# Two layers in one kernel: branch and query orders changed, two experts' weights asked for earlier, norm weights put on turned rows

## The chip, the core and the metric

The kernel runs on one core of one Trainium2 chip. A core has TensorE (matrix products), VectorE, ScalarE and GpSimd (elementwise work), SyncE (issues transfers), an on-chip memory of 128 partitions, eight accumulation banks (PSUM) that TensorE writes, and 16 DMA engines. The engines run their own instruction streams in order and wait for each other by semaphores. The metric is the time of one execution in microseconds (us) on the device; of several runs the median is given.

## The reference, cut to what matters

The program is two layers on 512 tokens of width 1024, in float32. The first layer is a block with a convolution branch, a block-sparse attention, an attention to a memory, and a gated feed-forward part; the change does not touch it. The second layer is this one:

```python
h = rms_norm(x, norm1_g)
z, xbc, dt_raw, q, k, v, g_ssd, g_att = split(h @ w_in)
xbc = silu(conv(xbc, 4 taps) + conv_b);  xs, bm, cm = split(xbc)
dt = softplus(dt_raw + dt_bias);  a = -exp(a_log)
# chunks of 128 tokens, 4 groups of 8 heads: sums of dt * a, states, y_diag + y_off + xs * d_skip
y_ssd = rms_norm(y * silu(z), per group) @ w_ssd_out
y_att = window_attention(rope(rms_norm(q)), rope(rms_norm(k)), v, sinks) @ w_attn_out
x = x + (sigmoid(g_ssd) * y_ssd + sigmoid(g_att) * y_att) @ w_out
h2 = rms_norm(x, norm2_g)
# router: one of 8 groups, the best 2 of its 8 experts; 64 experts
y = sum over the 2 experts of weight * (silu(h2 @ w_gate) * (h2 @ w_up)) @ w_down     # width 256
out = x + y
```

`rms_norm(x, g)` is `x / sqrt(mean(x^2) + eps) * g`, so the factor `g` (one number for each of the 1024 columns) can be put on rows that are already scaled by their root, before or after they are turned.

## The kernel before, in words

All dense products are made from three products of rounded halves: a weight `w` is split into a rounded high part and a rounded rest, and so are the activations; `product` (L512 to L515) adds high x high, high x low and low x high. A "tile" is 8 such products of 128x128 by 128x512, so 24 matmuls. ScalarE rounds the high part of a piece of weights (`one_hi`, L2156), VectorE subtracts it for the low part (`one_lo`, L1260). Both are done ahead of use, in the fixed order of the list `parts`: `highs.upto(e, n)` and `lows.upto(e, n)` bring the rounding up to part n at the place in the engine's program where they stand. There is no scheduler: the order on each engine is the order of the code in the functions `tensor`, `vector`, `scalar`, `pool` and `sync`. PSUM banks are taken in turn, and TensorE waits for whoever has to empty a bank.

The second layer on TensorE: tiles `bm0` to `bm3`; the product for dt (a 128-column piece), its turning by four transposes (L826); tiles `cm0` to `cm3`; the sums of dt * a over a chunk (L833 to L835). Then four groups g: tiles `xs{g}` 0 to 3, each followed by a turning of the tile before (`xs_rows`, L843), the rows of z, and the chunks' products (L870, L881, L920); the last chunk of a group is handled after the first xs tile of the next (`turn`, L851). Each bm, cm and xs tile passes ScalarE (L2335, scale and bias), VectorE (L1507, three taps) and ScalarE again (L2340, Silu). dt passes VectorE (L1578, copy), TensorE, VectorE (L1582) and ScalarE (L2408 to L2414, softplus in three functions, and an exponential), then VectorE. `chunk_rows` (L1654 to L1675) and `finish` on VectorE, and `finish` (L2426, the square) and `turn` (L2431) on ScalarE close a chunk.

Then q0, q1 and kv: row blocks i = 0 to 3 of 128 tokens, each over four quarters u of the weights, with a bank for each i; ScalarE copies q0 and q1 out (L2498), VectorE the rest (L1754). The angles of the rotary part are made on VectorE and their sine on ScalarE (L2490). Gate tiles `gs`, attention, output products `so` and `ao`, and the last projection `oo` (out in two halves of columns, L1927 adds it to X) follow.

The last stage is the experts. Each of the 64 experts gets 64 places for tokens; two experts make a block, so there are 32 blocks. The rows of h2 are written to memory (`h2d`) and gathered by an indirect transfer; TensorE turns them (L1197), VectorE (L2092) and ScalarE (L2663) copy a half each, and TensorE multiplies by gate and up weights (L1218) and by down weights (L1241). Weights come straight from memory, 2 MB of gate and up and 1 MB of down for an expert, into six places each (`GUs`, `DNs`); `gates_in(n)` and `downs_in(n)` in `sync` ask for them. `gates_in(0)` waits for the last projection's last products, `("oo", 3, 1)`; from expert 6 on, it waits for the block that last used the place. Expert 5's gate weights also wait for the routing's results. In `pool`, `row_3` (L2820) multiplies a row block of h2 by the gains of the norm and writes it out.

The lines that the change touches stand in these functions:

## Time and profile before

| | us |
|---|---|
| median of 3 runs | 2140.6 (2140.24 to 2140.8) |
| the profiled execution | 2140.07, of it 2138.2 span |
| TensorE busy | 1992.2 (93%) |
| VectorE busy | 1019.0 (48%) |
| ScalarE busy | 723.0 (34%) |
| GpSimd busy | 230.2 (11%) |
| chain that ended last | TensorE 67%, DMA 16%, VectorE 11% |

The span is the time from the first to the last instruction of the profiled execution. A busy share is an average over all stages. Rows of the timeline give the start and the length of one instruction or of a run of like ones, and in brackets how long the engine had been idle and what ended that. Overlapping matmuls are pipelined: their starts give the pace. Windows give the granted clock of TensorE as a share of 2.4 GHz.

### The profile page before, as it was taken

The page shows a single profiled execution, that of the slowest core. Times are in us where ns is not written, and L with a number is a line of the kernel's source. Part 1 is how long each engine was busy: PE and PEld are TensorE (multiplying, and loading weights), DVE is VectorE, ACT ScalarE, POOL GpSimd, SP SyncE. Part 2 cuts the span into 40 slices and gives each one's busy share as a digit, 9 for nine tenths or more (in the row PEclk, how much of TensorE's full clock was granted, in tenths as well). Part 3 has the DMA queues.
Part 4 walks back from the last instruction along what each step waited for, and adds up shares of the span by engine and source line. Part 5 has one row for each costly group of instructions (what it writes and reads, how often), then busy time and mean ns, then how long its engine had stood idle before and what let it go on. Part 6 is the DMA issues. An engine that isn't in the chain of part 4 may idle for free.

```text
span 2138.2 us, 23312 instructions
## 1 busy us (share of the span) xinstructions
PE 1992.2 (93%) x9626; PEld 1422.7 (67%) x9626; DVE 1019.0 (48%) x1596; ACT 723.0 (34%) x1156; POOL 230.2 (11%) x273
## 2 busy tenths in 40 slices
PE   7999999999999999899999999999987988888886
PEld 6777788888888888777787766678883332332222
DVE  4466534447666523678888457654353111111113
ACT  5353423235444412555554325652231110010000
POOL 2000000002000001101111141200023111111110
PEclk9999999999999999999999999999997999999999
DMA  7241123243222332332223221122429999999995
GB/s 267 89 137 61 59 83 114 79 165 122 99 99 99 118 118 99 107 126 94 75 99 123 88 79 40 60 99 79 148 103 411 422 423 424 423 424 421 419 412 212
DMA packets 56858, 380.46 MB, mean 178 GB/s; under 512 B 12936, under 2 KB 13192, under 8 KB 23856
## 3 DMA queue, kind: packets, MB, share of 16 engines
q1 hardware_dynamic: 38304, 339.23, 40.9%
q0 software_dynamic: 17872, 38.68, 5.1%
q8 instruction: 76, 1.25, 0.2%
q10 hardware_dynamic: 576, 1.05, 0.1%
q14 instruction: 30, 0.25, 0.0%
HBM read 378.82 MB, written 27.89 MB: 190 GB/s over the span
## 4 chain that ended last, share of the span: by engine, by line
PE 67%; DMA 16%; DVE 11%; ACT 3%; POOL 1%; issue 1%; SPq 0%; DVEq 0%; POOLq 0%; ACTq 0%
PE PS L513 17%; PE PS L515 17%; PE PS L514 17%; DMA AR<-in_wexp 15%; PE PS L1218 5%; PE PS L976 3%; DVE rf L1260 1%; PE PS L1241 1%; DVE AR L1625 1%; DVE AR L1507 1%; DVE AR L1618 1%; PE PS L1028 1%; PE PS L1058 1%; ACT rf L2156 1%; POOL AR L2685 1%
## 5 line engine op out<-in xcount | busy, mean ns | idle before, releaser
L513 PE MATMUL PS<-rf,rf 128*128 128x512 f32 (+1 forms) x2008 | 766.2, 382 | 20.6 <-DVE rf L1260 16.7
L514 PE MATMUL PS<-rf,rf 128*128 128x512 f32 (+1 forms) x2008 | 754.6, 376 | 0.0
L515 PE MATMUL PS<-rf,rf 128*128 128x512 f32 (+1 forms) x2008 | 754.6, 376 | 0.0
L1260 DVE TENSOR_TENSOR rf<-AR,rf 128x1024 fp32r<-128x1024 f32 (+1 forms) x224 | 285.6, 1280 | 365.4 <-ACT rf L2156 365.4
L513 PEld LDWEIGHTS PS<-rf,rf 128*128 128x128 f32 x2008 | 380.3, 189 | 97.0 <-DVE rf L1260 15.3
L515 PEld LDWEIGHTS PS<-rf,rf 128*128 128x128 f32 x2008 | 380.2, 189 | 68.6
L514 PEld LDWEIGHTS PS<-rf,rf 128*128 128x128 f32 x2008 | 380.6, 190 | 67.2 <-issue 1.2
L2156 ACT ACTIVATE rf<-AR 128x1024 fp32r<-128x1024 f32 (+1 forms) x224 | 244.1, 1100 | 265.9 <-PE PS L515 212.5
L1218 PE MATMUL PS<-AR 128*64 128x512 f32 x1024 | 272.9, 644 | 51.3 <-DMA AR<-in_wexp 50.0
L1218 PEld LDWEIGHTS PS<-AR 128*64 128x64 f32 x1024 | 86.3, 147 | 232.2 <-issue 160.0
L2101 DVE TENSOR_TENSOR AR<-AR,PS 128x256 f32<-128x256 f32 x32 | 13.5, 421 | 360.8 <-ACT AR L2674 360.8
L1241 PE MATMUL PS<-AR 128*64 128x512 f32 x512 | 116.9, 598 | 16.5 <-DVE AR L2105 16.5
L2674 ACT ACTIVATE AR<-PS 128x256 f32<-128x256 f32 x32 | 12.3, 384 | 298.3 <-PE PS L1218 298.3
L1241 PEld LDWEIGHTS PS<-AR 128*64 128x64 f32 x512 | 33.9, 136 | 79.0 <-issue 54.8
L976 PE MATMUL PS<-AR 128*128 128x512 f32 x160 | 70.7, 596 | 0.0
L1507 DVE SCALAR_TENSOR_TENSOR AR<-PS,AR 128x511 f32<-128x511 f32 (+2 forms) x72 | 53.8, 747 | 18.1 <-ACT AR L2335 16.5
L2680 ACT ACTIVATE AR<-PS 128x512 f32<-128x512 f32 x32 | 19.1, 597 | 127.1 <-PE PS L1241 127.1
L2836 POOL DMA_INDIRECT AR<-h2d,IA x32 | 32.7, 1023 | 268.1 <-PE PS L1227 248.1
L2685 POOL TENSOR_SCALAR AR<-AR 128x1 f32<-128x1 f32 (+1 forms) x46 | 24.6, 536 | 322.5 <-ACT AR L2308 119.2
L976 PEld LDWEIGHTS PS<-AR 128*128 128x128 f32 x160 | 29.7, 190 | 35.7 <-issue 35.6
L2109 DVE COPY AR<-PS 128x512 f32<-128x512 f32 x32 | 22.1, 692 | 65.3 <-PE PS L1241 65.3
L1197 PEld LDWEIGHTS PS<-AR 128*128 128x128 f32 x256 | 28.1, 143 | 32.7 <-issue 25.1
(331 smaller groups left out, 1791.6 us busy)
## 6 DMA issues: line engine op xcount, KB each, us to landing
AR<-in_wexp SPq DMA_DIRECT2D x62, 2048.0 KB, 35.9
AR<-in_wpack SPq DMA_DIRECT2D x123, 1024.0 KB, 5.0
AR<-in_wexp SPq DMA_DIRECT2D x68, 1024.0 KB, 38.2
AR<-acud POOLq DMA_DIRECT2D x16, 512.0 KB, 4.0
AR<-ya SPq DMA_DIRECT2D x4, 1024.0 KB, 8.7
bvec<-bv POOLq DMA_DIRECT2D x1, 2560.0 KB, 16.0
AR<-in_x SPq DMA_DIRECT2D x4, 512.0 KB, 7.3
AR<-bvec POOLq DMA_DIRECT2D x8, 256.0 KB, 2.9
```

The source lines that it names most:

```text
L513: e.i.matmul(o, ws[0], xs[0], start=start, stop=False)
L514: e.i.matmul(o, ws[0], xs[1], start=False, stop=False)
L515: return e.i.matmul(o, ws[1], xs[0], start=False, stop=stop)
L976: m = e.i.matmul(PS[:, b, :], w[:, d, :], YT[:, d, :], start=d == 0, stop=d == 15)
L1197: m = e.i.transpose(PS[:, b, 128 * k:128 * k + 128], XB[:, s, 512 * hf + 128 * k:512 * hf + 128 * k + 128], ident)
L1218: m = e.i.matmul(PS[CAP * j:CAP * j + CAP, b, :], xt[:, k, CAP * j:CAP * j + CAP], w[:, k, :], start=k == 0, stop=k == 7)
L1241: m = e.i.matmul(PS[CAP * j:CAP * j + CAP, b2[hf], :], hd[:, q, CAP * j:CAP * j + CAP], w[:, q, 512 * hf:512 * hf + 512], start=q == 0, st ...
L1260: e.i.tensor_tensor(rounded(p.place + p.width, p.width), src, rounded(p.place, p.width).bitcast(F32), ALU.subtract).then_inc(*tick("w_lo", ...
L1507: e.i.scalar_tensor_tensor(out=y[:, q:512], in0=b[:, 0:512 - q], scalar=cp("conv_w", 24 * (3 - q) + tix), in1=y[:, q:512], op0=ALU.mult, o ...
L2156: e.i.activation(rounded(p.place, p.width), area(p.chunk.place + p.off, p.width), ACT.Copy).then_inc(*tick("w_hi", p.key))
L2685: e.i.tensor_scalar(ss, ss, 1.0 / width, EPS, ALU.mult, ALU.add).then_inc(*tick("p_out", (key, "eps")))
L2836: e.i.indirect_dma_start(XB[:, s, :], None, dram["h2d"], bass.IndirectOffsetOnAxis(ap=IA[:, 128 + blk:129 + blk], axis=0), bounds_check=51 ...
```

## The change

Six places change.

- On TensorE, tile `cm0` moves ahead of the turning of dt, and `rows` (q0, q1, kv) asks for the bank of a row block when it comes to it, not for all four at the start.
- On VectorE, the copy of dt's product moves ahead of the fourth bm tile's taps, and the rest of dt's steps are spread over cm0 and cm1. On ScalarE, softplus moves from ahead of cm0 to behind it, and the exponentials of the sums (L2420) from behind cm3 to behind the second xs tile.
- In groups 1 to 3, both engines round the third xs piece right behind the first xs tile; ScalarE then turns before it squares.
- The sine moves behind the copies of q0, and two more pieces of the gate weights are rounded ahead of kv's copies.
- The gates and downs of expert 0 are asked for after `("ao", 7)`, the last products before the last projection, and those of expert 1 after the last rounded weights. The places of the experts' weights are laid out anew, over memory that is out of use by then.
- GpSimd no longer multiplies h2 by the norm's gains (four operations and a transfer of 0.5 MB go). VectorE and ScalarE multiply the turned rows by them instead, where they copied; ScalarE does this in four operations for each block.

```diff
@@ rows (tensor)
-                bs = []
-                for i in range(n):
-                    b, was = banks.take((name, i), back(i))
-                    bs.append(b)
-                    if was:
-                        e.wait_ge(*at(*was))
+                bs = [banks.take((name, i), back(i)) for i in range(n)]
...
-                    for i in range(n):
+                    for i, (b, was) in enumerate(bs):
                         c = slice(128 * i, 128 * i + 128)
+                        if was and u == 0:
+                            e.wait_ge(*at(*was))
@@ tensor
             m.then_inc(*tick("acc", "dt"))
+            conv_tile("cm", 0, 20)
             b, was = banks.take("dtt", ("v_out", "dtb"))
...
-            for j in range(4):
+            for j in range(1, 4):
                 conv_tile("cm", j, 20 + j)
@@ vector
+                if j == 3:
+                    e.wait_ge(*at("acc", "dt"))
+                    e.i.tensor_copy(D0, ps("dt")).then_inc(*tick("v_out", "d0"))
                 conv_taps("bm", j, 16 + j, BT[:, j, :])
-            e.wait_ge(*at("acc", "dt"))
-            e.i.tensor_copy(D0, ps("dt")).then_inc(*tick("v_out", "d0"))
...
             for j in range(4):
                 lows.upto(e, min(PART["cm", j] + 4, PART["xs0", 0] + (0 if j < 3 else 3)))
                 conv_taps("cm", j, 20 + j, CT[:, j, :])
+                if j == 0:
+                    e.wait_ge(*at("acc", "dtt"))
+                    e.wait_ge(*at("rows"))
+                    e.i.tensor_tensor(cut(DT, 4), cut(ps("dtt"), 4)[:, :, 0:32], h32("dt_bias"), ALU.add).then_inc(
+                        *tick("v_out", "dtb"))
+                if j == 1:
+                    steps()
...
                     if j == 0 and g:
+                        lows.upto(e, base + 4)
                         chunk_rows(g - 1, 3)
...
-                lows.upto(e, min(PART["kv", u] + 4, PART["gs0", 0]))
+                lows.upto(e, min(PART["kv", u] + 4, PART["gs0", 0] + 2))
...
-            e.wait_ge(*at("p_out", ("h2", 3)))
             e.i.tensor_scalar(CNT, ps("count")[:, 0:64], -float(CAP), 0.0, ALU.add, ALU.max).then_inc(*tick("v_out", "cnt"))
...
-                e.i.tensor_copy(xt[:, 0:4, :], cut(ps(("xt", blk, 0)), 4)).then_inc(*tick("v_out", ("xt", blk, 0)))
+                e.i.tensor_tensor(xt[:, 0:4, :], cut(ps(("xt", blk, 0)), 4), g4, ALU.mult).then_inc(
+                    *tick("v_out", ("xt", blk, 0)))
@@ scalar
+                    if j == 1 and g == 0:
+                        sums_raised()
                     if j == 0 and g:
+                        highs.upto(e, base + 4)
+                        turn(g - 1, 2)
                         finish(g - 1, 3)
-                        turn(g - 1, 2)
...
-            e.wait_ge(*at("v_out", "ang"))
-            e.i.activation(SIN, R1, ACT.Sin).then_inc(*tick("a_out", "sin"))
-            e.i.activation(COS, R1, ACT.Sin, scale=0.5).then_inc(*tick("a_out", "cos"))
...
+                if s == 0:
+                    ahead("q1", 0)
+                    e.wait_ge(*at("v_out", "ang"))
+                    e.i.activation(SIN, R1, ACT.Sin).then_inc(*tick("a_out", "sin"))
+                    e.i.activation(COS, R1, ACT.Sin, scale=0.5).then_inc(*tick("a_out", "cos"))
...
-                e.i.activation(xt[:, 4:8, :], cut(ps(("xt", blk, 1)), 4), ACT.Copy).then_inc(*tick("a_out", ("xt", blk, 1)))
+                for q in range(4):
+                    m = e.i.activation(xt[:, 4 + q, :], ps(("xt", blk, 1))[:, 128 * q:128 * q + 128], ACT.Copy,
+                                       scale=cp("norm2_g", 4 + q))
+                m.then_inc(*tick("a_out", ("xt", blk, 1)))
@@ pool
-            e.wait_ge(*at("v_out", ("ga2", 15)))
-            e.i.dma_start(GB, dram["gains"][2:3, :].to_broadcast([128, 1024])).then_inc(*tick("gains", 2, 16))
...
                 e.wait_ge(*at("a_out", ("hx", i)))
-                e.wait_ge(*at("gains", 2))
-                e.i.tensor_tensor(XR[i], XR[i] if i < 3 else SQ3, GB, ALU.mult).then_inc(*tick("p_out", ("h2", i)))
-                e.wait_ge(*at("p_out", ("h2", i)))
                 e.i.dma_start(dram["h2d"][128 * i:128 * i + 128, :], XR[i]).then_inc(*tick(f"st{i}", "h2", 16))
@@ sync
-                e.wait_ge(*at("acc", ("gu", n // 2 - 3) if n > 5 else ("oo", 3, 1)))
+                if n == 0:
+                    e.wait_ge(*at("acc", ("ao", 7)))
+                elif n == 1:
+                    e.wait_ge(*at("w_hi", ("oo1", 1)))
+                    e.wait_ge(*at("w_lo", ("oo1", 1)))
+                else:
+                    e.wait_ge(*at("acc", ("gu", n // 2 - 3) if n > 5 else ("oo", 3, 1)))
```

The order of instructions shows three places. The first is ScalarE from the fourth bm tile to the second cm tile. `rf<-AR` is a rounding of weights, `AR<-PS,AR` the entry of a conv tile, `AR<-AR 128x512` its Silu; the rows of 128x128 and 128x32 are dt's. Before:

```order
L2335 ACTIVATE AR<-PS,AR 128x512 [waits s_acc]
L2340 ACTIVATE AR<-AR 128x512 [waits s_v_out]
L2408 ACTIVATE AR<-AR 128x128 [waits s_v_out]
L2410 ACT_TABLE_LOAD
L2410 ACTIVATE AR<-AR 128x128 [waits s_a_out]
L2412 ACT_TABLE_LOAD
L2412 ACTIVATE AR<-AR 128x128 [waits s_a_out]
L2414 ACT_TABLE_LOAD
L2414 ACTIVATE AR<-AR 128x32 [waits s_rows]
L2156 ACTIVATE rf_1024<-AR 128x1024
L2335 ACTIVATE AR<-PS,AR 128x512 [waits s_acc]
L2340 ACT_TABLE_LOAD
```

In the changed kernel, whose lines are numbered some 8 higher (L2421 is L2408 before):

```order
L2164 ACTIVATE rf_1024<-AR 128x1024
L2343 ACTIVATE AR<-PS,AR 128x512 [waits s_acc]
L2348 ACTIVATE AR<-AR 128x512 [waits s_v_out]
L2421 ACTIVATE AR<-AR 128x128 [waits s_v_out]
L2423 ACT_TABLE_LOAD
L2423 ACTIVATE AR<-AR 128x128 [waits s_a_out]
L2425 ACT_TABLE_LOAD
L2425 ACTIVATE AR<-AR 128x128 [waits s_a_out]
L2427 ACT_TABLE_LOAD
L2427 ACTIVATE AR<-AR 128x32 [waits s_rows]
L2343 ACTIVATE AR<-PS,AR 128x512 [waits s_acc]
L2348 ACT_TABLE_LOAD
```

The softplus steps and their three tables now stand behind the first cm tile's Silu, and a rounding and that tile stand ahead of them.

The second place is ScalarE at the boundary between groups 0 and 1, from the Silu of the first xs tile (128x512 behind a table) to the Silu of the second. L2426 (L2437) is the last chunk's square, L2431 (L2442) a turned chunk's copy. Before:

```order
L2340 ACTIVATE AR<-AR 128x512 [waits s_v_out]
L2426 ACTIVATE AR<-AR 128x512 [waits s_v_out]
L2431 ACTIVATE AR<-PS 128x4x128 [waits s_acc]
L2156 ACTIVATE rf_1024<-AR 128x1024 [waits s_w_in1]
L2335 ACTIVATE AR<-PS,AR 128x512 [waits s_acc]
L2340 ACTIVATE AR<-AR 128x512 [waits s_v_out]
```

In the changed kernel:

```order
L2348 ACTIVATE AR<-AR 128x512 [waits s_v_out]
L2164 ACTIVATE rf_1024<-AR 128x1024 [waits s_w_in1]
L2442 ACTIVATE AR<-PS 128x4x128 [waits s_acc]
L2437 ACTIVATE AR<-AR 128x512 [waits s_v_out]
L2343 ACTIVATE AR<-PS,AR 128x512 [waits s_acc]
L2348 ACTIVATE AR<-AR 128x512 [waits s_v_out]
```

The rounding has gone from behind the square to ahead of it, and the turned chunk's copy too.

The third place is SyncE's queue from the first of the experts' transfers to the seventh expert's; 128x4096 are gates, 128x2048 downs. Before:

```order
L2916 DMA AR<-in_wexp 128x4096 [waits s_acc]
L2916 DMA AR<-in_wexp 128x4096
L2925 DMA AR<-in_wexp 128x2048 x2
L2916 DMA AR<-in_wexp 128x4096 x2
L2925 DMA AR<-in_wexp 128x2048 x2
L2916 DMA AR<-in_wexp 128x4096
L2925 DMA AR<-in_wexp 128x2048 x2
L2916 DMA AR<-in_wexp 128x4096 [waits s_v_out]
L2916 DMA AR<-in_wexp 128x4096 [waits s_acc]
```

In the changed kernel (L2936 is `gates_in`, L2945 `downs_in`):

```order
L2936 DMA AR<-in_wexp 128x4096 [waits s_acc]
L2945 DMA AR<-in_wexp 128x2048
L2936 DMA AR<-in_wexp 128x4096 [waits s_w_lo,s_w_hi]
L2945 DMA AR<-in_wexp 128x2048
L2936 DMA AR<-in_wexp 128x4096 [waits s_acc]
L2936 DMA AR<-in_wexp 128x4096
L2945 DMA AR<-in_wexp 128x2048 x2
L2936 DMA AR<-in_wexp 128x4096
L2945 DMA AR<-in_wexp 128x2048 x2
L2936 DMA AR<-in_wexp 128x4096 [waits s_v_out]
L2936 DMA AR<-in_wexp 128x4096 [waits s_acc]
```

Experts 0 and 1 now have waits of their own, and the wait for the last projection stands ahead of expert 2. The waits for the routing (`s_v_out`, expert 5) and for block 0 (`s_acc`, expert 6) stand where they stood.

## Rows read from the trace of the kernel before

**Rows 1.** The page, part 4: shares of the chain that ended last, by engine.
```profile
PE 67%; DMA 16%; DVE 11%; ACT 3%; POOL 1%; issue 1%; SPq 0%; DVEq 0%; POOLq 0%; ACTq 0%
```

**Rows 2.** Windows: from:to, length, each engine's busy us, granted clock, DMA share, GB/s.
```profile
1545.00:1590.00 45.00, 45.00 (x383) 45.00 (x382) 17.50 (x40) 13.42 (x17) 8.27 (x10) 1.00 0.09 34
1590.00:1635.00 45.00, 22.48 (x155) 14.07 (x154) 28.17 (x96) 6.96 (x11) 18.40 (x18) 0.62 0.96 390
1700.00:2080.00 380.00, 321.10 (x1362) 114.88 (x1360) 49.73 (x96) 36.90 (x70) 47.33 (x47) 0.95 1.01 421
```

**Rows 3.** TensorE's timeline (start, us, line, form, idle before); a row of waits.
```profile
895.99 1.12 PE L826 MATMUL PS<-AR 128*128 128x128 f32 x4 [6.23 <-DVE AR L1578]
...
1064.39 0.79 PE L513 MATMUL PS<-rf,rf 128*128 128x512 f32 x1 [2.90 <-DVE rf L1260]
...
1208.93 0.47 PE L513 MATMUL PS<-rf,rf 128*128 128x512 f32 x1 [2.86 <-ACT AR L2498]
...
1256.42 0.47 PE L513 MATMUL PS<-rf,rf 128*128 128x512 f32 x1 [2.07 <-DVE rf L1260]
...
PE PS L513 <- DVE rf L1260: 12.4, 5, 2.9
```

**Rows 4.** Windows over three stretches that follow a wait of TensorE.
```profile
895.00:902.00 7.00, 6.01 (x21) 5.00 (x22) 1.75 (x5) 5.08 (x7) 0.00 (x0) 0.66 0.00 0
1064.00:1074.00 10.00, 9.61 (x34) 7.80 (x35) 7.43 (x9) 4.16 (x4) 0.00 (x0) 0.68 0.44 138
1206.00:1215.00 9.00, 6.14 (x21) 4.86 (x21) 1.90 (x5) 3.24 (x7) 0.00 (x0) 0.81 0.29 96
```

**Rows 5.** ScalarE's timeline at dt and the cm tiles.
```profile
897.47 0.31 ACT L2408 ACTIVATE AR<-AR 128x128 f32<-128x128 f32 x1 [1.47 <-DVE AR L1582]
...
902.34 0.23 ACT L2414 ACTIVATE AR<-AR 128x32 f32<-128x32 f32 x1
...
909.36 0.78 ACT L2335 ACTIVATE AR<-PS,AR 128x512 f32<-128x512 f32 x1 [1.64 <-PE PS L515]
...
914.80 0.78 ACT L2335 ACTIVATE AR<-PS,AR 128x512 f32<-128x512 f32 x1 [1.64 <-PE PS L515]
...
918.50 3.79 ACT L2156 ACTIVATE rf<-AR 128x1024 fp32r<-128x1024 f32 x3
```

**Rows 6.** VectorE's timeline at the boundary between groups 0 and 1.
```profile
998.47 1.22 DVE L1260 TENSOR_TENSOR rf<-AR,rf 128x1024 fp32r<-128x1024 f32 x1 [2.22 <-ACT rf L2156]
```

**Rows 7.** Timeline at q0 and at the last products of kv: ScalarE, VectorE.
```profile
1206.38 0.23 ACT L2490 ACTIVATE AR<-AR 128x32 f32<-128x32 f32 x1 [2.92 <-DVE AR L1743]
...
1255.06 2.35 DVE L1260 TENSOR_TENSOR rf<-AR,rf 128x1024 fp32r<-128x1024 f32 x2
```

**Rows 8.** Timeline of the last projection and the first expert transfers.
```profile
1564.46 2.47 DVE L1927 TENSOR_TENSOR AR<-AR,PS 128x512 f32<-128x512 f32 x4
...
1624.60 10.98 SPq L2916 DMA_DIRECT2D AR<-in_wexp  x3
```

**Rows 9.** Timeline of the routing: VectorE and GpSimd.
```profile
1594.12 2.23 DVE L1941 TENSOR_SCALAR AR<-AR 128x64 f32<-128x64 f32 x1
...
1596.90 2.79 DVE L1935 SCALAR_TENSOR_TENSOR AR<-AR 128x64 f32<-128x64 f32 x1
...
1602.16 0.28 DVE L1935 SCALAR_TENSOR_TENSOR AR<-AR 128x64 f32<-128x64 f32 x1
...
1597.24 2.35 POOL L2820 TENSOR_TENSOR AR<-AR 128x1024 f32<-128x1024 f32 x1
```

**Rows 10.** Block 0 on TensorE; steps of the chain; a group of ScalarE.
```profile
1625.18 9.55 PE L1218 MATMUL PS<-AR 128*64 128x512 f32 x32 [1.29 <-DVE AR L2092]
...
1640.28 6.89 PE PS L1218 x32
...
1652.70 6.89 PE PS L1218 x32
...
L2663 ACT ACTIVATE AR<-PS 128x512 f32<-128x512 f32 x29 | 17.3, 597 | 18.5 <-PE PS L1197 18.5
```

79 lines of the change are left out of this document (43 added, 36 removed).

## The prediction

> **What bounds the kernel now.** I read the page first, then the timeline of TensorE, then the stretches by window. The chain that ended last [rows 1] is two thirds TensorE and one sixth transfers of the experts' weights. The reader should see two regimes. Up to 1591 us TensorE is busy nearly all the time, so any wait of TensorE there is worth its own length, if nothing else holds it afterwards. From 1591 us the experts' weights stream: in 1700 to 2080 the DMA share is 1.01 at 421 GB/s [rows 2], while TensorE waits. There a faster engine is worth nothing. Only a stream that starts earlier, carries less or stands still less counts. The profiled execution's 2140.07 us are a span of 2138.2 and 1.9 around it; the median of the runs, 2140.6, lies 0.5 above.
>
> The waits of TensorE that the change touches are [rows 3]: 6.2 us before the turning of dt (L826), waits for rounded weights (12.4 us in five; three of them are like the one at 1064.39, 2.9 us ahead of the third tile of a group's branch), 2.9 us before q1 (ended by ScalarE, L2498) and 2.1 us before the first gate tile. After some of them TensorE is granted half its clock (1.2 of 2.4 GHz) for a while. One minus the granted clock, times the stretch, gives the loss [rows 4]: 2.4 us after L826 (0.5 of it before the products start), 3.2 after the second group, 1.7 after q0.
>
> **dt and the cm tiles.** After the dt product TensorE (free at 895.99 - 6.23 = 889.8) now does cm0, one tile of 24 products, 5.4 us (two tiles' results reach ScalarE at 909.36 and 914.80 [rows 5]), and finds D0 copied: VectorE copies it ahead of the fourth bm tile's taps. So 6.2 + 1.9 of slow clock = 8.1 us go at the place. But ScalarE is late next. Its steps for dt (L2408 to L2414, 897.47 to 902.57, 5.1 us [rows 5]) now stand between cm0 and cm1. A turn of a tile over ScalarE, VectorE and ScalarE again takes 3.8 us (from 909.36 to 914.80 less 1.64 idle). The fourth bm tile was through ScalarE at 897.47 - 1.47 = 896.0 and is now at 896.6, with D0's copy ahead of it. From there: one rounding 1.0, cm0 3.8, dt 5.1, cm1 3.8, cm2 3.8, which is 914.1. Before, the same point, the three roundings for xs0 and z0 (3.79 us), stands at 918.50. So ScalarE gains 4.4 us and TensorE, whose cm tiles, turning and sums are done at about 913 (889.8 + 4 x 5.4 + 1.3), waits until 916 to 917 for xs0's weights, again at half clock for a while. The steps on the sums (L2420 on, with a table) move past two conv tiles and come due where ScalarE is late again, ahead of the rounding for xs0's last tile. I take 4 us, nearest the ScalarE row; the ends are 1 (the wait comes back nearly whole) and 8.
>
> Here the Trainium skill's page "ScalarE: Activation LUTs", section "What ACT_TABLE_LOAD costs", speaks against it: 1.28 us for a load and about as much again for draining, 2.66 in all. By that the three loads would make the steps 8 us and more, and the gain of this part would be about nothing, which is 2121.5 us. The whole stretch [rows 5] took 5.1 us with its three loads, so the trace shows no such second half, and the sum goes by it; the page's case has 0.02 of the chance of rival (1).
>
> **The group boundaries.** In groups 1 to 3 the rounding for the third xs tile now stands ahead of the last chunk's rows on VectorE, and ahead of the turn and the square on ScalarE. Before, VectorE idles 2.2 us for it after those rows (998.47 [rows 6]). At the place 2.9 us go three times, with 3.2 us of slow clock once. But the last chunk's rows and its square come later: VectorE stands about 1.8 us (an estimate: one small operation and one rounding of 1.0 on ScalarE) ahead of them, and 1.5 us afterwards, until ScalarE has squared and begun the next tile. So the next taps end 1 us later than before, and the fourth tile's rounding hangs on them. The wait moves one tile on. Where the clock had held (group 1) I expect nothing, even -0.3; in group 2, where TensorE had run slow for most of a tile, 2.4; in group 3 1.3; and about 1 us back for slow clock after the moved waits. Together 2.5, nearest the row in which VectorE, not TensorE, is the late one. The ends are -3 (1 us later in each group) and 12 (three times 2.9 and the 3.2).
>
> **q0, q1 and the gate tile.** ScalarE's copies of q0 stood behind a sine that waited 2.9 us for the angles [rows 7], and q1 waited for all four banks at once. Now the copies follow each row's product and q1 asks for a bank when it comes to it. Rows end 1.4 us apart (a quarter of a tile's 5.4) and a copy of this size takes 0.6 (as L2663 [rows 10]), so nothing is late: 2.9 + 1.7 of slow clock, 4.5 us. What queues behind the sine now is VectorE's rounding for q1's last quarter, due 3 x 5.4 us after q1's start. The two roundings at 1255.06 [rows 7] move ahead of the copies of k and v, under kv's products: 2.1 us, and no slow clock followed. Bounds for both together: 4 and 7.
>
> **The tail.** An expert is 128 x 6144 x 4 bytes, 3.15 MB. Two experts, 6.3 MB, now go at about 1536 (after ao7) and at 1564.5, when the last projection's weights are rounded [rows 8], where the mean is 34 GB/s over 1545 to 1590 [rows 2]. At the stream's 421 GB/s that is 14.9 us. SyncE's wait for those weights holds nothing else: all earlier loads are issued. X comes back beside the first expert; 5.2 MB in all are 12.5 us, done by 1551, ahead of the first add to X at 1564.46 [rows 8].
>
> The stream can't simply end 14.9 us earlier, because there are six buffers. The seventh expert waits for the first block's products, and those for the routing. Before: up to 1635, 45 us x 390 GB/s = 17.6 MB were moved [rows 2] of about 20.6 asked for (six experts 18.9, two rows of h2 1.0, small ones 0.7). So 3.0 MB, 7.2 us, still stood in line when block 0 ended and the seventh was asked for (the last of the three issues that begin at 1624.60 [rows 8]), and the stream never stood. After: about 14 MB are done by 1626, except for the sixth expert, which waits for the routing and is asked for at about 1620. Then nothing is left to ask for.
>
> How long nothing is left depends on the routing, and this is where the norm weights come in. Two VectorE operations on 128x64 take 2.23 and 2.79 us while GpSimd multiplies a row of h2 by the gains (1597.24, 2.35 us); the same operation takes 0.28 for the next row [rows 9]. Those multiplications go. 2.0 + 2.5 = 4.5 us leave VectorE's chain, which is what TensorE's routing products wait for. Block 0, 9.6 us from 1625.18 at a clock that rises late [rows 10], then ends at 1630.3 instead of 1634.8. The stream has no line then, and takes up again some 2 us later, at 1632.3. Before, at 1634.7, there were 7.2 us more to do. The gain is 7.2 + 2.4 = 9.6; I take 9.5. The ends: 5, if the 4.5 us of VectorE do not go, and 15, if the stream never stands.
>
> The weights on turned rows cost VectorE a product instead of a copy (0.1 us) and ScalarE four small copies instead of one of 0.6 us (L2663 [rows 10]): between +0.1 and +1.8 us (four at the price of the large one). TensorE's own pace is 12.4 us a block [rows 10], the stream's about 15.5 to 16, so this hides under the stream, and costs 0 to 2 us for all blocks together. I take 0.
>
> **The sum.** 4 + 2.5 + 4.5 + 2.1 + 9.5 = 22.6. Against the profile's own 2140.07 this gives 2117.5 us.
>
> **Rivals.** (1) The branch gives little: ScalarE and VectorE, not TensorE, set the pace from dt to the last group, so the first two parts give 1 and 0 instead of 6.5. For it speaks VectorE's idle time being ended by ScalarE [rows 6]; against it that TensorE runs nearly full between the boundaries. 2123. (2) The routing isn't shortened, since the stretched operations had another cause: 5 instead of 9.5, 2122; with (1), 2127.5. (3) The line of transfers doesn't run dry, or asked-for work spreads so that it hardly stands: 15 instead of 9.5, 2112. Against it, the six buffers. (4) The other side: scaling the turned rows. TensorE can't begin a block before ScalarE's half is written. If the four small operations and the product added more than 3.3 us to a block, TensorE would set the pace instead of the stream; from 4.2 us on, 32 blocks x 0.9 give back 29 of the 22.6 gained, and the kernel is slower, 2146. The nearest row, 0.6 us for the large copy, is against it: four such add 1.8. (5) The early transfers change nothing, because the first block isn't waiting for weights and the stream stands as long as it was relieved: the tail gives 0, 2127.
>
> **Chances.** The forecast 0.50 (own range 2112 to 2122); (1) 0.17, (2) alone or with (1) 0.10, (3) 0.11, (5) 0.07, (4) 0.03, no change at all, where two of the terms are paid back in full, 0.02. A measurement of this kernel tells about 0.2%, 4 us, from no change. Faster by more: 0.95; within: 0.02; slower: 0.03. The range, 2109 to 2128, leaves out (4), no change, and the ends of (3) and (2).
>
> **What would show it.** In the changed kernel's profile: no wait before the turning of dt, and one of 3 to 4 us before xs0's first tile; the 2.9 us waits gone from the second tile of a group and found again, as short ones, at the fourth; q1 following q0 at full clock; 3.15 MB moved after ao7, and again before the last rows; no VectorE operation of 2 us in the routing, and block 0 starting some 4.5 us sooner after the last projection; a hole in the DMA share of 4 to 8 us just before block 0 ends; from there 1.01 to the end. The forecast is wrong if the hole isn't there, if the group boundaries keep all of their 2.9 us, or if TensorE waits for ScalarE's half of the turned rows.

## The result, and the profile after

The changed kernel took 2116.9 us (median of 4 runs, 2116.5 to 2118.6) against 2140.4 for the kernel before on the same chip (2139.5 to 2140.8): a ratio of 0.9891, 95% interval 0.9877 to 0.9906. The profiled execution took 2116.47 us, its span 2114.7. On a second chip the medians were 2115.7 and 2138.6. The forecast was 2117.5, in a range of 2109 to 2128.

Where the 23.5 us of span went is read from instructions of TensorE that both traces have: the first product of the bm tiles, the first turning of a chunk in each group (L851 before, L850 here), the first scores of the attention (L1028 and L1027), which come behind kv and the first gate tiles, and the first product of the last projection. From the bm tiles to the first turning of group 0: 4.0 us less (110.5 for 114.4). From there to the same turning of group 3, three groups: 2.9 less. From there to the scores: 7.0 less. From the scores to the last projection nothing (244.9 us in both). From the last projection to the end: 9.6 less. The forecast had 4, 2.5, 6.6 and 9.5.

The chain that ended last is made up nearly as in [rows 1] (part 4 of the page):
```profile
PE 66%; DMA 17%; DVE 11%; ACT 4%; POOL 1%; issue 1%; SPq 0%; DVEq 0%; POOLq 0%; ACTq 0%
```
TensorE's timeline, at the places of [rows 3] (start, us, line, form, idle before). The lines L513, L1260 and L843 of before are L514, L1259 and L842 here.
```profile
916.19 0.54 PE L514 MATMUL PS<-rf,rf 128*128 128x512 f32 x1 [3.63 <-DVE rf L1259]
...
937.12 0.47 PE L514 MATMUL PS<-rf,rf 128*128 128x512 f32 x1 [1.32 <-DVE rf L1259]
...
999.52 0.66 PE L842 MATMUL PS<-AR 128*128 128x128 f32 x4 [1.28 <-ACT AR L2348]
...
1001.73 0.70 PE L514 MATMUL PS<-rf,rf 128*128 128x512 f32 x1 [0.89 <-DVE rf L1259]
```
No wait of 0.6 us or more stands between 868 and 916: the 6.2 us before the turning of dt are gone, and xs0's first tile now waits 3.6. Ahead of the third tile of a group nothing waits; at its end 1.3 and 0.9 us do, in all three groups. q1 and the gate tile have no wait of 0.6 us or more. What became of the slow clock of [rows 4] is seen in windows (length, busy us of the engines, granted clock, DMA share, GB/s) of the changed kernel, two at the same stretches and one, 999 to 1009, at the wait that is new:
```profile
895.00:902.00 7.00, 7.00 (x35) 5.82 (x34) 4.35 (x7) 3.29 (x6) 0.00 (x0) 1.00 0.33 97
999.00:1009.00 10.00, 8.56 (x33) 6.63 (x34) 7.43 (x9) 5.95 (x7) 0.00 (x0) 0.83 0.62 218
1206.00:1215.00 9.00, 9.00 (x41) 7.47 (x40) 2.18 (x2) 1.06 (x1) 0.00 (x0) 1.00 0.42 144
```
The clock is full after dt and after q0. It has fallen for a while after the wait ahead of xs0 (0.66 granted over 916 to 921) and after the new wait in group 1.

ScalarE's timeline answers to [rows 5]: the roundings for xs0 and z0, which began at 918.50, begin 4.7 us sooner.
```profile
901.79 1.28 ACT L2423 ACT_TABLE_LOAD   x1
...
906.33 0.23 ACT L2427 ACTIVATE AR<-AR 128x32 f32<-128x32 f32 x1
...
913.84 3.79 ACT L2164 ACTIVATE rf<-AR 128x1024 fp32r<-128x1024 f32 x3
```
The Trainium skill ("ScalarE: Activation LUTs", section "What ACT_TABLE_LOAD costs") gives 1.28 us for a load, and about as much again for draining. The first figure is what this row has to the digit. Of the second nothing is seen: the load that starts at 901.79 ends at 903.07, the next operation starts at 903.09, and the steps for dt took 5.1 us with three loads, as before.

The tail, in the windows that answer to [rows 2]:
```profile
1531.00:1577.00 46.00, 46.00 (x391) 46.00 (x391) 16.81 (x44) 13.43 (x17) 3.49 (x8) 1.00 0.39 155
1577.00:1622.00 45.00, 24.75 (x166) 14.96 (x166) 24.73 (x95) 8.82 (x18) 14.68 (x17) 0.66 0.88 343
1690.00:2060.00 370.00, 314.41 (x1345) 113.43 (x1340) 49.04 (x95) 48.87 (x138) 46.45 (x46) 0.95 1.01 421
1610.00:1615.00 5.00, 5.00 (x20) 1.72 (x18) 0.00 (x0) 0.00 (x0) 3.78 (x5) 0.72 0.59 240
1615.00:1620.00 5.00, 4.48 (x26) 1.94 (x24) 1.38 (x3) 1.53 (x5) 1.90 (x3) 1.00 0.58 141
1620.00:1625.00 5.00, 5.00 (x26) 1.73 (x24) 0.69 (x1) 0.60 (x1) 0.83 (x2) 1.00 1.00 417
```
46 us x 155 GB/s are 7.1 MB moved beside the last projection, where 34 GB/s (1.5 MB) went before. Then the stream runs full, falls to a share of 0.59 and 0.58 from 1610 to 1620 (0.41 and 0.42 of 5 us, 4.2 us lost: this is the hole), and runs at 1.01 to the end of the stretch at 2060.

Block 0, against [rows 10], with the steps that lead to it. The lines are, in this order: the last store of h2, the time from issue to landing of the one store issued in 1581 to 1583, the tokens' last operation, the fetch of block 0's rows, the turning of those rows, the block's products.
```profile
1581.47 0.53 POOL L2836 DMA_DIRECT2D h2d<-AR  x1 [0.92 <-ACT AR L2652]
...
h2d<-AR POOLq DMA_DIRECT2D x1, 512.0 KB, 14.3
...
1591.63 0.18 DVE L2014 TENSOR_SCALAR IA<-IA 128x32 int32<-128x32 int32 x1
...
1596.81 1.13 POOL L2850 DMA_INDIRECT AR<-h2d,IA  x1 [14.80 <-DVE AR L2044]
...
1605.15 1.97 PE L1196 MATMUL PS<-AR 128*128 128x128 f32 x8 [9.18 <-DMA AR<-h2d,IA]
...
1608.40 9.27 PE L1217 MATMUL PS<-AR 128*64 128x512 f32 x32 [1.28 <-issue]
```
The routing reached TensorE 4.5 us sooner after the last projection (L1158 at 1586.23; L1159 at 1604.69 before). But block 0 began only 2.8 us sooner (1608.40, where 1625.18 less 14.0 is 1611.2). The tokens were there at 1591.8, and the fetch was issued at 1596.8, when the last store had landed: it was issued at 1581.47 and took 14.3 us, so it landed at 1595.8. This is a wait that the forecast did not have. The profile names a VectorE operation as what ended the fetch's wait; in the code the fetch waits for the four stores and for the tokens, not for that operation.

The wait is not new. In the kernel before, the last store landed at 1610.6 (1599.89 and 10.7), the fetch left as long after that as it does now, and the products began 3.3 us after the turning, as they do now (1605.15 to 1608.40):
```profile
1599.89 0.59 POOL L2822 DMA_DIRECT2D h2d<-AR  x1 [0.30 <-POOL AR L2820]
1611.67 1.13 POOL L2836 DMA_INDIRECT AR<-h2d,IA  x1 [11.19 <-DVE AR L2022]
...
1621.92 1.97 PE L1197 MATMUL PS<-AR 128*128 128x128 f32 x8 [7.48 <-DMA AR<-h2d,IA]
```
So before, two chains ended nearly together at block 0: the routing on VectorE, which was free at 1624.3 to copy its half, and store, fetch and turning, whose rows were ready at 1623.9. The change took 4.1 us off the first. The second lost 2.8: the store is issued 4.4 us sooner after the last projection, but takes 3.6 longer to land, and the fetch is 1.9 shorter. In one of the runs below (six passes) the chain has the step itself, store and then fetch:
```profile
1580.92 14.21 DMA h2d<-AR
1596.18 8.18 DMA AR<-h2d,IA
```

### The profile page after: what moved, and what is told of

Its sections match the earlier page's. It is cut to its first block, busy times and chain, and to the rows that moved or that the text cites. A ratio compares the mean times of both kernels' runs of the same rounds, so it can differ in the third digit from the quotient of the medians.

```text
span 2114.7 us, 23398 instructions
## 1 busy us (share of the span) xinstructions
PE 1985.4 (94%) x9626; PEld 1418.8 (67%) x9626; DVE 1012.9 (48%) x1596; ACT 739.8 (35%) x1252; POOL 220.8 (10%) x268
## 3 DMA queue, kind: packets, MB, share of 16 engines
q10 hardware_dynamic: 576, 1.05, 0.1%
## 4 chain that ended last, share of the span: by engine, by line
PE 66%; DMA 17%; DVE 11%; ACT 4%; POOL 1%; issue 1%; SPq 0%; DVEq 0%; POOLq 0%; ACTq 0%
PE PS L514 17%; PE PS L516 17%; PE PS L515 16%; DMA AR<-in_wexp 15%; PE PS L1217 5%; PE PS L975 3%; DVE AR L1506 2%; DVE rf L1259 2%; PE PS L1240 1%; DVE AR L1631 1%; ACT rf L2164 1%; PE PS L1027 1%; PE PS L1057 1%; POOL AR L2704 1%; DVE AR L1624 1%
## 5 line engine op out<-in xcount | busy, mean ns | idle before, releaser
L514 PE MATMUL PS<-rf,rf 128*128 128x512 f32 (+1 forms) x2008 | 763.9, 380 | 13.2 <-DVE rf L1259 12.2
L1259 DVE TENSOR_TENSOR rf<-AR,rf 128x1024 fp32r<-128x1024 f32 (+1 forms) x224 | 285.8, 1281 | 368.5 <-ACT rf L2164 368.4
L514 PEld LDWEIGHTS PS<-rf,rf 128*128 128x128 f32 x2008 | 379.2, 189 | 89.0 <-DVE rf L1259 13.6
L1506 DVE SCALAR_TENSOR_TENSOR AR<-PS,AR 128x511 f32<-128x511 f32 (+2 forms) x72 | 53.8, 747 | 17.4 <-ACT AR L2343 15.7
```

The lines of the kernel that those rows point to most:

```text
L514: e.i.matmul(o, ws[0], xs[0], start=start, stop=False)
L1259: e.i.tensor_tensor(rounded(p.place + p.width, p.width), src, rounded(p.place, p.width).bitcast(F32), ALU.subtract).then_inc(*tick("w_lo", ...
L1506: e.i.scalar_tensor_tensor(out=y[:, q:512], in0=b[:, 0:512 - q], scalar=cp("conv_w", 24 * (3 - q) + tix), in1=y[:, q:512], op0=ALU.mult, o ...
```

## The experiments

Each but one is the changed kernel with an edit. The tail below is the span less the start of the last projection; without an edit it is 591.7 and 592.0 us in two profiles. The runs were spread over three chips. The kernel before had a median of 2138.2 us on the chip of the first four edits (experts late, gains, dt, all groups), 2138.6 on that of q0, the repeat, four passes and halves, and 2139.0 on that of group 1 alone, six passes and the two with the stores; its single runs spread from 2134 to 2142. Of these the changed kernel itself was run on the second only, so its stages and its tail, which agree within 0.3 us in two profiles, say more than the times do.

**Experts 0 and 1 asked for late.**
```
-                if n == 0:
-                    e.wait_ge(*at("acc", ("ao", 7)))
-                elif n == 1:
-                    e.wait_ge(*at("w_hi", ("oo1", 1)))
-                    e.wait_ge(*at("w_lo", ("oo1", 1)))
-                else:
-                    e.wait_ge(...)
+                e.wait_ge(*at("acc", ("gu", n // 2 - 3) if n > 5 else ("oo", 3, 1)))
```


> The changed kernel with experts 0 and 1 asked for where the kernel before asks for them, after the last projection's weights of the fourth row; all else stays changed. The forecast's account (the 9.6 us of the tail come from 6.3 MB moved ahead, less a hole): the stages up to the last projection stay 14.0 us sooner, the stream's line starts as before and does not run dry before block 0 ends, so the tail gives nothing: 2140.4 - 14 = 2126 to 2127, and the DMA share has no hole there. Rival (5), the first block's start sets the tail, whatever was moved ahead: block 0 still starts about 3 us sooner relative to the last projection, so the time stays at 2117 to 2119, or gives back at most half.

Measured: 2125.5 us (2125.0 to 2125.8), 0.9942 [0.9925, 0.9960] of before. The tail is 601.7 us, where before has 601.3. There is no hole (share 1.05, and 0.98 in the 5 us after):
```profile
1610.00:1615.00 5.00, 5.00 (x12) 1.52 (x14) 0.00 (x0) 1.11 (x1) 3.78 (x5) 0.50 1.05 418
```
So the whole gain of the tail hangs on the early transfers. That the routing is 4.5 us faster is worth nothing by itself: the stream still has a line when block 0 ends. Rival (5) falls.

**GpSimd multiplies h2 by the gains again.**
```
+                e.i.tensor_tensor(XR[i], XR[i] if i < 3 else SQ3, GB, ALU.mult)...
-                e.i.tensor_tensor(xt[:, 0:4, :], cut(ps(("xt", blk, 0)), 4), g4, ALU.mult)...
+                e.i.tensor_copy(xt[:, 0:4, :], cut(ps(("xt", blk, 0)), 4))...
```
(The gains are fetched again too, and ScalarE copies its half in one operation again.)

> The changed kernel with GpSimd multiplying h2 by the norm's gains again, as before, and the turned rows only copied (the fourth row's square and scaled row go to an area of their own, as before). The forecast's account: two VectorE operations in the routing take 2.2 and 2.8 us again, TensorE's routing products come 4.5 us later, block 0 ends 3 to 4 us later, and the hole in the stream grows from about 4 to 7 or 8 us: 2116.9 + 3 to 4.5 = 2120 to 2121.5. Rival: since the fetch of block 0's rows waits in the changed kernel for the stores of h2 to land and not for the routing, the multiply costs next to nothing: within 1 us of 2116.9. Rival (2), the stretched operations had another cause: they stay short and the time stays.

Measured: 2119.9 us (2119.8 to 2122.0); the tail is 596.4 us, 4.4 to 4.7 more. VectorE and GpSimd (whose span is rough), and two windows:
```profile
1578.97 2.22 DVE L1949 TENSOR_SCALAR AR<-AR 128x64 f32<-128x64 f32 x1
...
1581.74 2.79 DVE L1943 SCALAR_TENSOR_TENSOR AR<-AR 128x64 f32<-128x64 f32 x1
...
1578.80 2.34 POOL L2837 TENSOR_TENSOR AR<-AR 128x1024 f32<-128x1024 f32 x1
...
1582.09 2.35 POOL L2837 TENSOR_TENSOR AR<-AR 128x1024 f32<-128x1024 f32 x1
```
```profile
1605.00:1610.00 5.00, 1.50 (x9) 1.09 (x8) 4.70 (x11) 1.88 (x2) 2.08 (x2) 0.50 0.16 62
...
1615.00:1620.00 5.00, 5.00 (x27) 1.86 (x24) 0.06 (x1) 0.38 (x1) 3.65 (x5) 1.00 0.26 85
```
The two long operations are back, each beside a multiply, and only there: rival (2) falls. The hole is in two pieces, 4.2 us and 3.7 (0.84 and 0.74 of 5 us), about 8 in all. The first comes from the sixth expert, whose gates are asked for when the routing has left its buffer: 1609.4 here, 1606.2 in the changed kernel, though that one's last projection starts 1.2 later: 4.4 us apart. The second comes from block 0, which begins 88.2 us after the start of the last projection, against 85.4 and 85.8 in the two profiles of the changed kernel: its turned rows wait 3.5 us for VectorE. So with the early transfers in place the 4.5 us count in full. Block 0 got only 2.4 to 2.8 of them; the sixth expert's request got nearly all. The time is at the lower edge of the forecast's account (2120 to 2121.5), and the rival by which the multiply costs next to nothing falls as well.

**The order of dt and the cm tiles undone.**
```
-            conv_tile("cm", 0, 20)
             b, was = banks.take("dtt", ("v_out", "dtb"))
             ...
-            for j in range(1, 4):
+            for j in range(4):
                 conv_tile("cm", j, 20 + j)
```
(and VectorE's and ScalarE's steps with it, the exponentials of the sums too)

> The changed kernel with dt, its turning, the cm tiles and the steps on the sums in the order of before. The forecast's account: TensorE waits 6.2 us ahead of the turning of dt again, at half clock afterwards, and does not wait 3.6 us ahead of xs0: the branch from dt on is 4.0 us later, 2121. Rival (1), ScalarE sets the pace from dt to the last group: the later stages catch up and the time stays within 1.5 us of 2116.9.

Measured: 2119.7 us (2119.6 to 2121.5). That is 18.4 below the kernel before on its chip, where the changed kernel is 22.9 and 23.5 below. From the first product of the bm tiles to group 0's first turning it takes 116.8 us, against 110.5 in the changed kernel and 114.4 in the kernel before: 6.3 more and 2.4 more. Nothing is caught up later: each later stage is within 0.3 us of the changed kernel's, and the tail is 591.7. (The last projection starts only 5.1 us later, because the program reached the bm tiles 0.95 us sooner here; over all the profiles that point lies between 855.1 and 856.5, whatever the edit.) Of rival (1) nothing is left for this part. The 2.4 us between this order and the same order in the kernel before are slow clock: the products behind the 6.2 us wait run slow from 894.91 to about 901, where those of before do so from 895.99 to about 900, and the clock falls once more (0.97 granted over 935 to 992, where before has 1.00). So this part gives 4.0 to 6.3 us, by how the clock falls in the old order.

**The group boundaries undone, all three, and only group 1's.**
```
                     if j == 0 and g:
-                        lows.upto(e, base + 4)
                         chunk_rows(g - 1, 3)
...
                     if j == 0 and g:
-                        highs.upto(e, base + 4)
-                        turn(g - 1, 2)
                         finish(g - 1, 3)
+                        turn(g - 1, 2)
```


> The changed kernel with the rounding for a group's third tile behind the last chunk's rows, the turn and the square, as before, in all three groups. The account by group (measured between the two traces as -1.4, +2.7, +1.6 us gained in groups 1, 2, 3): group 1 gets 1.4 us faster, groups 2 and 3 2.7 and 1.6 slower: 2116.9 + 2.9 = 2120. Rival (1) has 0 for this part: 2117. A second rival, that the gain in groups 2 and 3 came from the dt part's new start and not from this order: group 1 gains 1.4, 2 and 3 keep what they have: 2115.5.

> The changed kernel with the new order at the group boundaries for groups 2 and 3 only; group 1's rounding stands behind the last chunk's rows, turn and square as before. By the comparison of the two traces (group 1 took 64.6 us before and 66.0 after) the new order costs there: 1.4 us back, 2115.5. By the run with all three boundaries undone (group 1 took 67.5 us in it) the new order gains 1.4 there and the trace of before was only spared the slow clock: group 1 at 67.5 us, and the time 2117 to 2118.

Measured: 2117.6 us (2116.5 to 2119.7) and 2116.3 (2115.4 to 2117.4). TensorE's rows at the three boundaries of the first, and at that of group 1 of the second:
```profile
995.60 0.80 PE L514 MATMUL PS<-rf,rf 128*128 128x512 f32 x1 [2.86 <-DVE rf L1259]
...
1063.06 0.79 PE L514 MATMUL PS<-rf,rf 128*128 128x512 f32 x1 [2.88 <-DVE rf L1259]
...
1129.27 0.50 PE L514 MATMUL PS<-rf,rf 128*128 128x512 f32 x1 [2.87 <-DVE rf L1259]
```
```profile
995.25 0.50 PE L514 MATMUL PS<-rf,rf 128*128 128x512 f32 x1 [2.89 <-DVE rf L1259]
```
The waits are the same, 2.9 us. What differs is the clock behind them: the first product takes 0.80 and 0.79 us in two, at half clock, and 0.50 in the others, as in group 1 of the kernel before:
```profile
999.74 0.50 PE L513 MATMUL PS<-rf,rf 128*128 128x512 f32 x1 [2.88 <-DVE rf L1260]
```
The length of a group (from the first turning of a chunk in one group to that in the next) follows the clock:

| kernel | group 1 | group 2 | group 3 | order |
|---|---|---|---|---|
| before | 64.6 | 67.4 | 66.2 | old |
| all undone | 67.5 | 66.2 | 64.6 | old |
| group 1 undone | 64.6 | 66.0 | 64.6 | old, new, new |
| changed | 66.0 | 64.8 | 64.6 | new |
| changed, again | 65.8 | 64.8 | 64.6 | new |

At full clock a group takes 64.6 us in the old order with its 2.9 us wait, and 64.6 to 64.8 in the new order without. The new order gives nothing there: TensorE's wait has moved to the tile's end. What differs is the size of the loss when the clock falls: 1.6 or 2.8 us behind the long wait, 1.0 to 1.4 behind the two short ones. The account from the comparison of the two traces (a loss of 1.4 us in group 1, gains of 2.7 and 1.6 in groups 2 and 3) was wrong in its parts: with all three undone, group 1 is 1.5 us longer, group 2 is 1.4 longer and group 3 is the same. Group 1 alone undone does come out at 64.6 us, as that account had it, but so it does at full clock in either order: it had been spared the slow clock, as in the kernel before. The times of these two runs can't tell a difference of 1 to 3 us from none; the reading rests on the profiles.

**q0 and q1 undone:** the sine ahead of q0's copies again, and the wait for all banks ahead of q1.
```
+            e.wait_ge(*at("v_out", "ang"))
+            e.i.activation(SIN, R1, ACT.Sin)...
...
+                for b, was in bs:
+                    if was:
+                        e.wait_ge(*at(*was))
```


> The changed kernel with the sine and cosine ahead of ScalarE's copies of q0 and the wait for all four banks ahead of q1, as before; the gate tile's earlier roundings stay changed. The forecast's account: TensorE waits 2.9 us ahead of q1 and runs 1.7 us slow after it: 4.5 of the measured 7.0 us of this stretch go, 2121.4. Rival: only the wait comes back, or the gate tile's part is larger than the 2.1 us forecast and holds the rest: 2119 to 2120.

Measured: 2121.4 us (2119.5 to 2123.6). The wait is back:
```profile
1203.51 0.47 PE L514 MATMUL PS<-rf,rf 128*128 128x512 f32 x1 [2.88 <-ACT AR L2513]
```
From group 3's first turning to the scores: 120.9 us, against 116.2 in the changed kernel and 123.2 before. So q0 and q1 gave 4.75 of the 7.0. The other 2.3 are left for the gate tile, which was not undone by itself. The last projection starts 6.3 us later; 1.1 of this is slow clock in group 3, and 0.5 lies ahead of the groups, nearly all of it ahead of the bm tiles. The tail is 592.5.

Group 1 of this run shows that the first product alone doesn't tell the clock. It takes 0.50 us here, the clock falls two products later, and the group takes 66.0 us, as in the changed kernel, whose first product took 0.70:
```profile
1002.21 0.50 PE L514 MATMUL PS<-rf,rf 128*128 128x512 f32 x1 [0.89 <-DVE rf L1260]
1002.55 0.48 PE L515 MATMUL PS<-rf,rf 128*128 128x512 f32 x1
1002.82 0.63 PE L516 MATMUL PS<-rf,rf 128*128 128x512 f32 x1
```

**The changed kernel again.**

> The changed kernel once more, as the reference for the others of this call: 2116.5 to 2117.5, every stage within 0.3 us of its first profile.

Measured: 2115.7 us (2114.0 to 2116.8). The bm tiles begin 0.4 us sooner than in the first profile, outside the 0.3 us expected; every stage from there to the last projection is within 0.15, and the tail of 592.0 is 0.3 longer.

**ScalarE's scaled copies four and six times over.**
```
+                for p in range(4):
+                    if p:
+                        e.wait_ge(*at("a_out", ("xt", blk, 1, p - 1)))
                     for q in range(4):
                         m = e.i.activation(xt[:, 4 + q, :], ...)
```


> The changed kernel with ScalarE's four scaled copies of turned rows done four times over in every block, each pass waiting for the one before: 3 x 1.14 = 3.4 us more per block and three short waits. Rival (4) tested from the far side: it said that 3.3 us more in a block turn the bound from the stream to TensorE, each further us costing 32. By it, TensorE's pace of 12.4 us a block plus 3.4 to 4.2 is 15.8 to 16.6 against the stream's 15.5, so the time is 2125 to 2150, and TensorE's waits for ScalarE's half show in every block. The other theory: ScalarE makes block n+1's half right after block n's silu, so the copies lie beside TensorE's other work or beside its wait for weights and need not be on its path: 2117 to 2119, and the price that rival (4) named was too high.

> The changed kernel with ScalarE's four scaled copies done six times over in every block, each pass waiting for the one before. With four passes (4.66 us for sixteen copies) TensorE's blocks in the stream came 13.85 us apart where it did not wait for weights, 1.4 more than 12.4, and still under the stream's 15.5. Theory: each pass now adds its full 1.2 us to a block, since ScalarE's copies end last before the next block's products; two more make 16.2, above the stream: about 24 blocks x 0.7 to 0.9 and 6 us on the first block, 2135 to 2150; TensorE then waits for ScalarE in every block and hardly for weights. Rival: the passes still lie beside other work, the pace is under 15.5, and only the first block's start shows: 2120 to 2124.

Measured: 2118.7 us (2117.7 to 2120.1) and 2166.8 (2166.4 to 2167.3), the latter 1.0132 [1.0115, 1.0149] of before. ScalarE's row of a block with four passes and with six:
```profile
1823.52 4.66 ACT L2683 ACTIVATE AR<-PS,AR 128x128 f32<-128x128 f32 x16 [0.64 <-PE PS L1196]
```
```profile
1825.12 7.03 ACT L2683 ACTIVATE AR<-PS,AR 128x128 f32<-128x128 f32 x24 [0.63 <-PE PS L1196]
```
The chain of waits of either (start, us, what): blocks that follow each other, with four passes, then with six.
```profile
1626.75 7.09 PE PS L1217 x32
1639.61 7.09 PE PS L1217 x32
```
```profile
1715.50 8.78 PE PS L1217 x32
1732.43 7.09 PE PS L1217 x32
1747.65 8.71 PE PS L1217 x32
...
PE PS L1217 <- ACT AR L2683: 57.0, 22, 2.6
```
With four passes ScalarE takes 4.66 us for its half instead of 1.14, and where TensorE doesn't wait for weights its blocks come 12.9 us apart instead of 12.4: of 3.5 us added, 3.1 cost nothing. (The 13.85 us that the expectation for six passes went by is no such pace: the changed kernel has blocks 13.9 us apart too.) What the tail lost, 3.6 to 3.9 us, it lost on block 0, which starts 3.6 to 4.0 later: there the whole addition counts. Six passes add 2.4 more, and now they count in full in every block: 15.2 us (1732.43 to 1747.65), of which TensorE waits 2.6. But most blocks come 16.9 apart (1715.50 to 1732.43), because the products behind the wait take 8.78 us instead of 7.09, at the slower clock (mean granted 0.91 over 1690 to 2060, 0.96 with four passes). 32 blocks of 12.4 us fit under the stream, and so do 32 of 12.9; 32 of 16.9 do not, TensorE is the bound to the end, and the kernel is slower than before. So rival (4) is a real mechanism, but neither its place nor its price was right. It had TensorE set the pace from 3.3 us added on, as if every added microsecond lengthened a block; with 3.5 added the blocks are 0.5 longer and the stream still sets the pace (share 1.01 over 1690 to 2060), because 3.1 us are hidden first. With 5.9 added its rule (12.4 + 5.9 = 18.3 against 15.7 a block, times 32) would give some 83 us more; measured are 50 more than the changed kernel. My 2135 to 2150 was too low, because it left out the slow clock, up to 1.7 us a block. Where between 3.5 and 5.9 us added the time turns was not tried. The change itself added 0.5.

**Experts 6 and 7 in halves; h2's store ahead of the line; both.**
```
+                    if blk == 0 and k == 3:
+                        m.then_inc(*tick("acc", "gu_half"))
...
+                if blk == 3:
+                    e.wait_ge(*at("acc", "gu_half"))
+                    for j in range(2):
+                        e.i.dma_start(area(GUs[j], 4096)[:, 0:2048], wexp[n + j, :, 0:2048])...
```
(the other halves of the two go where the whole ones went)
```
+                if n == 3:
+                    e.wait_ge(*at("st3", "h2"))
```
(and block 1's weights are asked for expert by expert)

> The changed kernel with the gate weights of experts 6 and 7 asked for in two halves: the first as soon as block 0's first four rounds of products have read their half of the buffers, instead of at the end of block 0's gate products. The forecast's account: the hole of about 4.2 us in the stream (share 0.59 at 1610 to 1620) is due to having nothing to ask for, so asking 3 to 4 us sooner fills most of it: 2113 to 2115. Rival: the end of the kernel is set otherwise, or the stream loses it again later: 2116.5 to 2117.5.

> The changed kernel with the weights of expert 3 and later asked for only once the fourth row of h2 is stored, and block 1's weights asked for expert by expert. Theory (from the changed kernel's trace): the fetch of block 0's rows, issued at 1596.8, waits for the last store of h2, issued at 1581.5, which lands 15 us later behind experts' transfers, while the routing had its tokens 5 us before; with fewer transfers in line the store lands sooner, block 0 starts 1 to 3 us sooner, and the hole shrinks: 2114 to 2116. Rival: the transfers held back leave the stream standing while the store travels, a new hole of some us: 2118 to 2122, though block 0 starts sooner. A third: the fetch isn't waiting for the store, and block 0 starts when it does now.

> The edits of the two runs before, halves and stores, together. If the store's theory holds and costs no new hole, 1 to 2 us below halves (2114.3 against 2115.7 for the changed kernel of the same chip): 2112 to 2113.5. If holding transfers back opens a hole, above halves: 2115 to 2119.

Measured: halves 2114.3 us (2113.2 to 2116.4; the changed kernel on the same chip 2115.7), stores 2115.7 (2115.5 to 2117.0), both 2114.4 (2113.2 to 2115.2), these two on the third chip. The tails are 589.7, 591.6 and 590.8 us. Windows of halves, then of stores:
```profile
1610.00:1615.00 5.00, 5.00 (x22) 1.74 (x20) 0.00 (x0) 0.00 (x0) 4.08 (x5) 0.88 0.58 191
1615.00:1620.00 5.00, 4.48 (x26) 2.00 (x24) 1.38 (x3) 1.52 (x5) 1.32 (x2) 1.00 0.99 410
```
```profile
1590.00:1595.00 5.00, 2.69 (x32) 2.43 (x31) 2.25 (x16) 0.33 (x2) 1.32 (x2) 0.50 0.55 170
...
1615.00:1620.00 5.00, 3.46 (x20) 1.54 (x18) 1.45 (x3) 1.53 (x5) 2.71 (x3) 1.00 0.82 289
```
Halves takes half of the hole away, 2.1 us, and the tail is 2.0 to 2.3 us shorter: the hole was a lack of things to ask for. It has the lowest median of all, but its runs overlap with those of the changed kernel, so "faster" rests on the profiles and not on the times. Stores shows two things. The store now lands 9.5 us after its issue instead of 14.3, and the fetch leaves at 1593.4, 4.0 us sooner after the last projection: it was the store that held it. But block 0 starts only 1.7 us sooner (at 1607.3, 83.8 us after the start of the last projection, for 85.4):
```profile
1601.60 1.97 PE L1196 MATMUL PS<-AR 128*128 128x128 f32 x8 [5.03 <-DMA AR<-h2d,IA]
...
1607.31 8.46 PE L1217 MATMUL PS<-AR 128*64 128x512 f32 x32 [3.74 <-DVE AR L2099]
```
its turned rows wait 3.7 us for VectorE, which is busy with the routing's last operations. And the stream stands 2.3 us while the store travels (0.55 at 1590). The hole has moved (of the 4.2 us at 1610 to 1620 0.9 are left), and the time is the same. Both edits together keep that hole and are no better than halves alone.

## Why the prediction was right, step by step

dt and the cm tiles: right, 4.0 against 4 (6.3 by the undone order, 2.4 of it slow clock that the kernel before had not met), the late one being ScalarE as forecast: 4.7 us sooner at the rounding for xs0, where 4.4 was worked out, and TensorE waiting 3.6.

The group boundaries: the sum right by luck (2.9 against 2.5), the step wrong. "At the place 2.9 us go three times" is true of the place and of nothing else, and the forecast's own remark that the wait moves one tile on was the whole of it. Rival (1)'s half, 0 for the order, is what holds at full clock. The 2.9 us are a difference of slow clock, 4.4 in before (2.8 + 1.6) and 1.5 after. So the sum hangs on how the clock fell in two traces: in the old order group 1 alone came out at 67.5 in one kernel and at 64.6 in two.

q0, q1 and the gate tile: right, 4.75 against 4.5, and 2.3 against 2.1, the latter by subtraction.

The tail: the sum right (9.6 against 9.5), by both of its parts. Early transfers without the faster routing give 4.9 (601.3 less 596.4, the lower end was 5), the faster routing without them nothing, both together 9.6. The step that was wrong: "4.5 us leave VectorE's chain", and so block 0 ends 4.5 us sooner. The 4.5 us did leave, but block 0 ended only 3.1 sooner (1617.6, where 1634.7 less 14.0 is 1620.7), since its rows wait for the store of h2 to land, then for the fetch, and that chain got only 2.8 shorter. The sixth expert was asked for as forecast: about 1620 on the time scale of before is 1606, and it was 1606.2. That the sum came out all the same is luck in part. The forecast had 14.9 us moved ahead and, with a gain of 9.6, 5.3 lost again. Read from the DMA share, it was some 14 us ahead after the first 75 us from the start of the last projection (0.61 for 0.43), and lost 4.7 in the next 25 (0.82 for 1.01), though block 0 ended 1.4 later than forecast, which should have made the loss larger. Two errors of about a microsecond cancel.

The scaled rows: as good as the 0 that was forecast. ScalarE's four copies take 1.14 us for 0.60, VectorE's product 0.684 for 0.683, as these two rows of the groups' table say. In the stream that is hidden. On block 0 it probably is not: the copies end at 1608.3, the products begin at 1608.40, and with four passes the whole addition came through there. So up to 0.5 us of block 0's late start is the scaling, an estimate, since it was not undone by itself.
```profile
L2099 DVE TENSOR_TENSOR AR<-PS,AR 128x512 f32<-128x512 f32 x32 | 21.9, 684 | 0.2 <-PE PS L1196 0.2
...
L2680 ACT ACTIVATE AR<-PS,AR 128x128 f32<-128x128 f32 x128 | 36.6, 368 | 34.7 <-PE PS L1196 34.7
```

## What to carry to other kernels

A comparison of two traces by stages has the slow clock in it; before a gain or loss of 1 to 3 us is put down to an order, look at the granted clock behind the wait in both (the first product alone can miss it, as group 1 with q0 undone shows), and measure a stage between two instructions that both traces have. Where a stream has a limited number of buffers, price an earlier start together with what frees the next buffer: here the two halves of the change gave 9.6 us together, the early transfers alone 4.9 and the shorter routing alone nothing. And when a chain is shortened, go through every wait of the instruction at its end, the stores that it depends on too, and not only the one that came last before. Here two chains ended within half a microsecond of each other, and only one was shortened by 4 us.

## What the runs showed of the hardware that was not expected

The same wait of 2.9 us at the same place of the same instructions was followed by half clock in one kernel's profile (0.80 us for the first product, all groups undone, group 1) and not in another's (0.50, group 1 alone undone). Two waits of 1.3 and 0.9 us were followed by it in 12 of 35 group boundaries of the new order. How long it stays there varied too: 13 products of 0.6 us and more in group 2 of the kernel before, 7 in its group 3.

A store of 512 KB took 14.3 us from issue to landing behind 10.5 MB asked for on another engine's queue in the 4.3 us before it, and 9.5 us behind 3.1 MB. It doesn't follow the line alone: in the kernel before, with more in line, the last two stores took 10.2 and 10.7. The cause is open.

Two VectorE operations of 64 elements a partition took 2.22 and 2.79 us beside GpSimd's multiplies of 2.34 and 2.35 us, and 0.25 and 0.28 without. That the multiplies go and the long operations with them was forecast; that the run with the multiplies back has them back at the same places shows it.
